# Experts in blocks of 1024 columns with deeper rings, and the low part of every weight chunk on VectorE alone

## The reference

```python
def _expert_choice_ffn(h, router_w, wg, wu, wd):      # per group; 16 experts, FF = 2048
    cap = EC_CAPACITY_FACTOR * n // N_EXPERTS         # 64 latent + 16 context rows per expert
    probs = jax.nn.softmax((h @ router_w).astype(jnp.float32), axis=-1)
    gate, idx = lax.top_k(jnp.swapaxes(probs, 1, 2), cap)
    xs = h[b_idx, idx]
    hid = silu(xs @ wg[e]) * (xs @ wu[e])
    ye = (hid @ wd[e]) * gate[..., None]
    return zeros_like(h).at[b_idx, idx].add(ye)
```

## Time and profile before

| what | us |
|---|---|
| median of three runs | 1772.27 (1772.03 to 1791.83) |
| the profiled execution | 1767.41 |
| its span, first to last instruction | 1765.4 |
| TensorE busy | 1557.6 |
| VectorE busy | 1235.6 |
| GpSimd busy | 1155.3 |
| ScalarE busy | 1000.3 |
| moved by DMA | 476.73 MB |

### The profile page before, as it was taken

One profiled execution on the slowest core, in us unless ns is written; L12 is line 12 of the kernel. 1 busy time (PEld: TensorE's weight loads), 2 busy tenths in 40 slices (PEclk: granted clock), 3 DMA queues, 4 the chain that ended last, 5 costly groups with the idle time before them and its releaser, 6 DMA issues.

```text
span 1765.4 us, 21080 instructions
## 1 busy us (share of the span) xinstructions
PE 1557.6 (88%) x7025; PEld 1059.3 (60%) x7025; DVE 1235.6 (70%) x1121; ACT 1000.3 (57%) x813; POOL 1155.3 (65%) x517
## 2 busy tenths in 40 slices
PE   5699987888848999999999999999999899999992
PEld 2588765556735556565656656566665565655661
DVE  5525554774565877788787877778878678887773
ACT  6223344243425666676766667667676676766761
POOL 5311231143116797897988989889797797977880
PEclk9699999989858999999999999999999999999996
DMA  9321113256225898999999999999999989989983
GB/s 343 105 72 48 48 49 98 84 174 236 106 107 214 325 357 316 347 348 342 364 344 367 342 339 361 335 377 339 341 376 333 354 329 350 363 330 357 335 317 126
DMA packets 189109, 476.73 MB, mean 270 GB/s; under 512 B 11406, under 2 KB 13706, under 8 KB 172684
## 3 DMA queue, kind: packets, MB, share of 16 engines
q1 hardware_dynamic: 177744, 447.77, 68.8%
q0 software_dynamic: 3728, 13.11, 3.0%
q10 hardware_dynamic: 7596, 15.30, 2.4%
HBM read 462.51 MB, written 13.64 MB: 270 GB/s over the span
## 4 chain that ended last, share of the span: by engine, by line
POOL 41%; issue 22%; PE 20%; DVE 7%; DMA 5%; ACT 4%; POOLq 0%; ACTq 0%; SPq 0%; DVEq 0%
POOL w_lo L256 37%; PE bank L287 3%; PE bank L288 3%; PE bank L286 3%; ACT w_hi L250 2%; POOL arena L1437 2%; DMA raw<-in_ada_w 2%; POOL gate_e L1433 1%; PE bank L852 1%; DVE w_lo L256 1%; PE bank L769 1%; PE bank L692 1%; DMA arena<-xn_rows,slot_e 1%; PE bank L899 1%; PE bank L900 1%
## 5 line engine op out<-in xcount | busy, mean ns | idle before, releaser
L256 POOL TENSOR_TENSOR w_lo<-raw,w_hi 128x384 fp32r<-128x384 f32 (+1 forms) x424 | 1032.1, 2453 | 512.5 <-ACT w_hi L250 507.6
L256 DVE TENSOR_TENSOR w_lo<-raw,w_hi 128x1664 fp32r<-128x1664 f32 (+1 forms) x424 | 902.3, 2139 | 379.0 <-ACT w_hi L250 376.8
L250 ACT CAST w_hi<-raw 128x2048 fp32r<-128x2048 f32 x424 | 806.5, 1910 | 340.8 <-PE bank L904 90.5
L899 PE MATMUL bank<-w_hi,act_lo 128*80 128x512 f32 x1024 | 410.9, 401 | 19.6 <-DVE act_lo L1337 19.5
L900 PE MATMUL bank<-w_hi,act_hi 128*80 128x512 f32 x1024 | 406.5, 397 | 0.0
L904 PE MATMUL bank<-w_lo,act_hi 128*80 128x512 f32 x1024 | 279.4, 394 | 3.9 <-POOL w_lo L256 3.7
L914 PE MATMUL bank<-w_hi,act_lo 128*80 128x512 f32 x512 | 204.3, 399 | 16.9 <-DVE act_lo L1348 13.8
L899 PEld LDWEIGHTS bank<-w_hi,act_lo 128*80 128x80 f32 x1024 | 155.9, 152 | 102.1 <-issue 21.9
L904 PEld LDWEIGHTS bank<-w_lo,act_hi 128*80 128x80 f32 x1024 | 151.8, 149 | 92.1 <-issue 9.8
L900 PEld LDWEIGHTS bank<-w_hi,act_hi 128*80 128x80 f32 x1024 | 153.8, 150 | 79.7 <-issue 2.8
L915 PE MATMUL bank<-w_hi,act_hi 128*80 128x512 f32 x512 | 201.1, 393 | 0.0
(11 more groups left out here) (208 smaller groups left out, 1400.9 us busy)
## 6 DMA issues: line engine op xcount, KB each, us to landing
raw<-in_exp_gate SPq DMA_DIRECT2D x128, 1024.0 KB, 5.4
raw<-in_exp_up SPq DMA_DIRECT2D x128, 1024.0 KB, 5.4
raw<-in_exp_down SPq DMA_DIRECT2D x128, 1024.0 KB, 5.8
raw<-in_ada_w SPq DMA_DIRECT2D x24, 1024.0 KB, 6.1
raw<-in_w_in SPq DMA_DIRECT2D x12, 1024.0 KB, 5.2
arena<-in_x_lat ACTq DMA_DIRECT2D x8, 512.0 KB, 9.1
raw<-in_w_out SPq DMA_DIRECT2D x4, 1024.0 KB, 7.5
xn_rows<-arena ACTq DMA_DIRECT2D x5, 512.0 KB, 2.7
```

The costliest lines, as they stand in the source:

```text
L250: nc.scalar.copy(w_hi[:, n % WS, :], raw[:, n % RAW, :]).then_inc(hi_done, 1)
L256: ops.tensor_tensor(w_lo[:, n % WS, at], raw[:, n % RAW, at], w_hi[:, n % WS, at], ALU.subtract).then_inc(done, 1)
L899: mm(dst, x[1][:, kk, :], wh[:, k, :], start=(kk == 0), stop=False)
```

## The change

1. `split_lo` is VectorE's alone, for all 2048 columns, in the prologue and in the experts. GpSimd keeps its other work there, and in the experts only copies columns, gathers and scatters.
2. For expert chunks the raw ring has 6 slots and the w rings 4. The added slots lie where xn2, h2T and the activations of the prologue are dead by then (`raw_more`, `w_hi_more`, `w_lo_more`); the fifth and sixth load wait for that.
3. The hidden width is worked in blocks of 1024: all expert chunks are two pieces x 1024 columns, in four parts per block. For gate and up the runs in memory become 4 KB instead of 2 KB. The body is now, four chunks each: g1 d0 u1 g0' d1 u0'. Gate uses banks 0 and 1, up 2 and 3, down 4 and 5.
4. All side work is placed anew. In the body of expert e, with chunks numbered 0 to 23 in that order: hidden transposes behind chunks 1, 2, 13 and 14; `gathered_T` behind chunks 4 and 7; `gathered` for the two halves behind VectorE's lo parts of chunks 9 and 12; ScalarE's `gathered_half` behind its hi parts of chunks 10 and 13; `gathered_lo` behind the lo parts of chunks 11 and 14; `ye` behind the hi parts of chunks 24 and 25 (0 and 1 of the next body). GpSimd does columns, gather and scatter with nothing between.

The number of matmuls, transposes and bytes stays as it is. The core of the diff follows: the constants, the order of chunks, loads and splits, then the bodies of TensorE, VectorE, ScalarE (its lines stand behind `split_hi(act, N_BODY + i + WS_X, e)`) and GpSimd.

```diff
 RAW, WS = 4, 3
+RAW_X, WS_X = 6, 4
-DVE_COLS, DVE_COLS_EXP = 1536, 1664
...
-        order = [("u", 1, 0), ("d", 0, 0), ("g", 2, 0), ("u", 2, 0), ("d", 1, 0), ("g", 3, 0), ("u", 3, 0), ("d", 2, 0)]
-        if not last:
-            order += [("g", 0, 1)]
-        order += [("d", 3, 0)]
-        if not last:
-            order += [("u", 0, 1), ("g", 1, 1)]
-        return [(kind, b, half, nxt) for kind, b, nxt in order for half in range(2)]
+        order = [("g", 1, 0), ("d", 0, 0), ("u", 1, 0)] + [("g", 0, 1)] * (not last) + [("d", 1, 0)] + [("u", 0, 1)] * (not last)
+        return [(kind, b, part, nxt) for kind, b, nxt in order for part in range(4)]
...
+        elif j == RAW:
+            sp_e.wait_ge(xn_out, 16 * TILES)
+            sp_e.wait_ge(h2_ps, 2 * TILES)
+        elif j == RAW + 1:
+            sp_e.wait_ge(sl_rd, 1)
+        else:
+            sp_e.wait_ge(lo_done, e * PER_E + (n - RAW_X + 1))
...
+        if n >= N_EXP + WS:
+            act.wait_ge(w_used, e * PER_E + (n - WS_X + 1))
...
+    def split_lo(dve, n, e=0):
+        dve.wait_ge(hi_done, e * PER_E + (n + 1))
+        nc.vector.tensor_tensor(w_chunk(w_lo, n), raw_chunk(n), w_chunk(w_hi, n), ALU.subtract).then_inc(lo_done, 1)
...
+                if part == 0:
+                    if kind == "g":
+                        pe.wait_ge(sl_ev, 4 * e + (4 if nxt else 2))
+                        if nxt:
+                            pe.wait_ge(xs_l, 2 * e + 4)
+                    elif kind == "u":
+                        pe.wait_ge(hid_rd, 4 * e + (4 if nxt else 2))
...
+                if kind == "g" and part in (1, 2):
+                    half = 2 * (1 - b) + part - 1
+                    if part == 2:
+                        pe.wait_ge(ht_lo, 4 * e + half)
+                    hid_T(e, half)
...
+                if not last and (kind, b, part) == ("d", 0, 0):
                     pe.wait_ge(xs_f, 2 * e + 2)
                     pe.wait_ge(xg_in, 16 * e + 32)
                     gathered_T(1 - pr2, 0)
+                if not last and (kind, b, part) == ("d", 0, 3):
                     pe.wait_ge(xs_f, 2 * e + 3)
                     gathered_T(1 - pr2, 1)
...
+                if kind == "u" and part == 3:
+                    for half in range(2):
+                        hidden(n, e, e + nxt, 2 * b + half)
...
+                if not last or i + WS_X < len(chunks):
+                    split_lo(dve, n + WS_X, e)
+                if not last and (kind, b, part) == ("d", 0, 1):
                     gathered(e + 1, 0)
+                if not last and (kind, b, part) == ("d", 0, 3):
                     gathered_lo(e + 1, 1 - pr2, 0)
+                if not last and (kind, b, part) == ("u", 1, 0):
                     gathered(e + 1, 1)
+                if not last and (kind, b, part) == ("u", 1, 2):
                     gathered_lo(e + 1, 1 - pr2, 1)
...
+                    if part == 2 and not last:
+                        gathered_half(e + 1, 1 - pr2, 0)
+                if not last and (kind, b, part) == ("u", 1, 1):
                     gathered_half(e + 1, 1 - pr2, 1)
+                if not last and (kind, b) == ("u", 0) and part < 2:
+                    ye_out(e, pr2, part, N_BODY + 19)
...
+            if not last:
+                pool.wait_ge(sl_ct, 1)
+                pool.wait_ge(ga_ps, 2 * e + 2)
+                pool.wait_ge(f_add, 16 * e + 16)
+                columns_of(e + 1, 1 - pr2, col_ct)
+                pool.wait_ge(sl_ct, 1)
+                pool.wait_ge(col_ct, 2 * e + 2)
+                gather(1 - pr2)
+            pool.wait_ge(sl_ct, 1)
+            pool.wait_ge(ye_rd, 2 * e + 2)
```

More of the change, by code:

```diff
@@ new lines, in body_chunks, with raw_chunk, w_chunk @@
+        return [(kind, b, part, nxt) for kind, b, nxt in order for part in range(4)]
+    FIRST_CHUNKS = [(kind, 0, part) for kind in "gu" for part in range(4)]
+    def raw_chunk(n):
+        if n < N_EXP:
+            return raw[:, n % RAW, :]
+        slot = (n - N_EXP) % RAW_X
+        return raw[:, slot, :] if slot < RAW else raw_more[slot - RAW]
+    def w_chunk(ring, n):
+        if n < N_EXP:
+            return ring[:, n % WS, :]
+        slot = (n - N_EXP) % WS_X
+        if slot == WS:
+            return w_hi_more if ring is w_hi else w_lo_more
+        return ring[:, (N_EXP + slot) % WS, :]
@@ L559, in _ @@
         split_hi(act, N_EXP + 2)
+        split_hi(act, N_EXP + 3)
         act.wait_ge(lg_sub, 1)
@@ L826, in _ @@
             chunk_ready(pe, n)
-            wh, wl = chunk_view(w_hi, n, 512), chunk_view(w_lo, n, 512)
+            wh, wl = cols(w_chunk(w_hi, n), 512), cols(w_chunk(w_lo, n), 512)
             for t in range(TILES):
@@ L890, in gathered_T, with products @@
             last.then_inc(ga_ps, 1)
-        def up_or_gate(n, e, bank, half, x):
-            dst = psum[bank][0:SLOTS, :]
-            wh, wl = chunk_view(w_hi, n, 512), chunk_view(w_lo, n, 512)
+        def products(n, e, banks, x, first, final):
+            wh, wl = cols(w_chunk(w_hi, n), D), cols(w_chunk(w_lo, n), D)
+            steps = [(j, q, slice(q * 512, (q + 1) * 512)) for j in range(2) for q in range(2)]
             pe.wait_ge(hi_done, e * PER_E + (n + 1))
-            for k in range(4):
-                kk = 4 * half + k
-                mm(dst, x[1][:, kk, :], wh[:, k, :], start=(kk == 0), stop=False)
-                mm(dst, x[0][:, kk, :], wh[:, k, :], start=False, stop=False)
+            for j, q, at in steps:
+                dst = psum[banks + q][0:SLOTS, :]
+                mm(dst, x[j][1], wh[:, j, at], start=(first and j == 0), stop=False)
+                mm(dst, x[j][0], wh[:, j, at], start=False, stop=False)
@@ L922, in hid_T, with up_or_gate, down @@
+        def up_or_gate(n, e, kind, part, x):
+            products(n, e, 0 if kind == "g" else 2, [[a[:, 2 * part + j, :] for a in x] for j in range(2)],
+                     part == 0, part == 3)
+        def down(n, e, b, part):
+            at = [slice((2 * (part % 2) + j) * SLOTS, (2 * (part % 2) + j + 1) * SLOTS) for j in range(2)]
+            products(n, e, 4, [[a[:, at[j]] for a in hidT[part // 2]] for j in range(2)],
+                     b == 0 and part == 0, b == 1 and part == 3)
         def hid_T(e, b):
@@ new lines, in body @@
+                if kind == "g" and part in (1, 2):
[3 more added lines that the diff above has]
+                    hid_T(e, half)
+                if last and (kind, b, part) == ("u", 1, 3):
+                    hid_T(e, 2)
+                    pe.wait_ge(ht_lo, 4 * e + 3)
+                    hid_T(e, 3)
+                if last and (kind, b, part) == ("d", 1, 1):
+                    pe.wait_ge(gbias2, 16)
+                    pe.wait_ge(sl_ev, 4 * NEXP)
+                    pe.wait_ge(hid_rd, 4 * NEXP)
+                    gate_rows(rows, (0, 1, 2, 3))
@@ L1371, in body @@
[L1371 to L1382 removed]
+            if last:
+                gate_row(4, (0, 1, 2, 3))
```

287 lines of the change are left out of this document (117 added, 170 removed).

## The result

The changed kernel is slower: 1825.59 us (median of four runs, 1818.35 to 1833.31) against 1772.15 before; the recorded ratio is 1.032, with a 95% interval of 1.027 to 1.037 (the two medians alone give 1.030). The forecast was 1765 us, with 1730 to 1792 as its range. The profiled execution took 1826.2 us, its span 1824.4: 59.0 more than before. The times in the table of experiments are medians over all executions, while the ratios leave out one slow execution of e2 (1783.7 us) and one of e8 (3897.3 us, without which its median is 1796.4).

The account below looks back on a forecast made before the run. TensorE was taken as the bound, 69.2 us per expert. With waits and clock 74.2 against 74.4: -3 over 15 experts, prologue -4, tail +1, giving 1761 from 1767.4; the run median lies 0.3% higher: 1765 us, range 1730 to 1792.

Parts of the forecast that it names:

- TensorE's floor: Expert loop: 24 chunks of matmuls plus six transpose sets bound each expert at 69.2 us.
- VectorE alone: Low parts wholly on VectorE: 2.29 us per chunk, 62 us per expert of 72 or more, so not the bound.
- the prologue: Before the expert loop: GpSimd's low parts fall away, VectorE's grow; sum -4 us, bounds -9 and +6.
- Waits at L1348: TensorE's waits for the low activations of hid, 12.5 us in the loop before; the new order removes them.
- First half of the gathered rows: TensorE's wait in each expert for VectorE to split this half: 0.5 us.
- Second half: TensorE's wait in each expert for the other half of the gathered rows: 2.95 us, or 2.3 without backlog.
- The clock: Slowed TensorE matmuls after a long wait: 1.1 us per expert (6 in 10 of 1.9), bounds 0 and 1.9.
- The gather: Rows for the next expert land in time by 1.7 us at the medians; 0.5 us per expert, bounds 0 and 3.2.
- t21: End of chunk 21 on TensorE; from it the gather was timed to land after 18.1 us, 18.6 with semaphores and start.
- The late case: Scatter and gather at longest landing plus 0.6 for a busy queue: rows come 3.2 us after TensorE wants them.
- The rival with the late gather: Gather comes late and the clock falls at both waits: 79.7 us per expert, 1848 us; chance 0.12.
- The floor of 72.1 us: DMA's estimated time per expert by the skill page's 358 GB/s; the forecast preferred 67.4 us from a measured 383 GB/s.

Follow-up runs that it names:

- e2: Changed kernel with each expert load issued as two, giving 2 KB runs for gate and up: 1769.2 us, ratio 0.996.
- e8: Changed kernel with four raw slots instead of six and loads in 2 KB runs: 1798.1 us, ratio 1.012.
- e6: Changed kernel with the gather issued one body earlier, ahead of the scatter's wait, and gathered-row work one to two chunks earlier: 1687.4 us, ratio 0.949.
- e3: Kernel before the change with only VectorE doing all 2048 columns of every low part; old rings, blocks and order: 1737.4 us, ratio 0.979.
- e5: Changed kernel with the gather issued one body earlier from its own index buffer, ahead of the scatter's wait: 1729.1 us, ratio 0.973.
- e9g: Changed kernel with one load per expert held back until the gather has landed: 1774.3 us, ratio 1.003.
- e10: Changed kernel with every low part issued as two instructions of 1024 columns instead of one of 2048: 1792.9 us, ratio 1.012.

## Why the prediction was wrong

- **TensorE's floor** of 69.2 us per expert was right: 68.80 in e6.
- **VectorE alone** at 2.29 us per chunk was right (2290 ns), and so was that VectorE doesn't bound the expert. What it frees was mis-sized. I took the prologue at -4; the first transposes came 5.1 us earlier, and 9.3 in e3. The 4 us between the two are the first gather: 519.25 to 527.20 in the changed kernel, 518.82 to 523.01 in e3, where no fifth and sixth load is issued at that point. In the old order alone it also takes 1.5 us off an expert. I had no sum for this part by itself, which is worth 35 to 38 us.
- **Waits at L1348** went, as said, and no wait of ScalarE for raw is left in the expert stage.
- **First half of the gathered rows**, 0.5 us: it isn't there. In e5, where no gather wait could cover it, TensorE doesn't wait at its second transposes, and they start 8.60 us behind the first, as in e6 (8.59), where this work stands earlier.
- **Second half**, 2.95 us taken: 2.2 and 0.17 ahead of it, 2.37 measured, in each expert. The value without backlog, 2.3, was the right one.
- **The clock**, 1.1 us per expert taken, 0 to 1.9 as bounds. Alone, a wait of 2.2 us costs the clock in few experts (four periods of 14 in e5). In the changed kernel it did so each time, and 13 of the 14 gather waits did too. The bounds of the term allowed one fall per expert; there were two.
- **The gather**, 0.5 us taken, is the step that failed, by the two landings in its line from t21. Its other terms were right. ye's second half is written at 1023.46, 2.7 us behind t21 (1020.77, from TensorE's steps; 2.8 taken), the scatter starts 0.87 later (0.8 taken), from the copies to the gather it is 1.17 (1.2 taken). For the landings I took 7.6 + 6.5 = 14.1; in this cycle they are 9.60 (1024.33 to 1033.93) and about 10.0 (1035.10 to just ahead of 1045.18): 5.5 more. With 14.1 TensorE would have had 1.5 us to spare (2.7 + 0.9 + 14.1 + 1.2 = 18.9 behind t21; it comes at 20.44, 1041.21). The difference, 4.0, is the wait of 3.97. The sign that I had named for this, a gather wait above 1 us, came.
- **A slip in the same line.** Its own terms, 2.8 + 0.8 + 7.6 + 1.2 + 6.5, add up to 18.9 and not to 18.1, and with the 0.5 for semaphores and start to 19.4: the slack was 0.9 us, not 1.7. The late case then is 4.0 us after TensorE and not 3.2, and the upper bound of the term was too low by as much; measured are 4.3 us on average in the loop. The slip alone would have left the gather in time at the medians; it hid how thin the margin was.
- **Why the landings were mis-sized.** I took them from a kernel in which GpSimd did low parts, and held them to be free of what this change alters. The runs put the gather's 3.5 us down to 0.3 for the instruction and 3.2 behind it; of these 2.0 are loads issued beside it (e9g takes them away). 2 KB runs give 1.2 (e2), which may be partly the same. For the scatter 0.7 of 2.2 are the instruction. Some 1.2 and 1.5 us stay open. My argument against this rival, that both medians were taken beside a full queue, was wrong in its first half: from the gather's start on no load went out for 3.6 to 4.5 of its 6.5 us.
- **The rival with the late gather** gave 79.7 us per expert and 1848; measured are 78.7 and 1826. It was the case that came, at a chance of 0.12, and by its own point: over 1.7 us above the medians. Its mechanism was right (landings at the longest seen or above, clock falling twice). That its number is so near is in part luck: it took 0.5 us that aren't there and 2.95 for 2.37, and had the gather's wait at 3.2 for 4.3. Its chance should have been far larger, since even the slack of 1.7 was 12% of a sum of times that were all seen with another engine setting the pace.
- Two rules of the Trainium skill stood beside the forecast. The floor of 72.1 us estimated from the first (DMA: Bandwidth & Descriptors, "Where 436 GB/s comes from") doesn't hold here: e6 runs at 68.80 us and 376 GB/s. So DMA was not the bound, as taken. The oscillating clock (TensorE: Matmul & The Clock Gate, "HAM oscillation") is what the changed kernel shows; in e5, with one wait in every iteration, the clock fell in four of 14.

## What to carry to other kernels

A landing time is a property of the kernel it was taken in. When an engine that paced the loads is relieved, other loads come to lie beside a small transfer; they were 2.0 of the gather's 3.5 us here. A chain whose slack is smaller than that wants a margin for it. Look at the chain itself first: a gather whose indices are known long before has no business behind a scatter, and moving it gave 96 us; the deeper ring was worth its 52 us only once TensorE waited for nothing, the longer runs nothing then. Take a change apart before judging it: its first part alone was worth 2.1%, the remainder cost 5% on top of it, and with both waits repaired the whole is 5.1% faster than before.

## What I hadn't expected of the hardware

- GpSimd's DMA_INDIRECT takes 1.00 us with VectorE idle, 2.4 to 3.1 beside one low part of 2048 columns, and 5.5 beside two; in three kernels (changed, e5, e10) it ended 0.87 to 0.88 us behind the end of a VectorE instruction.
- A scatter-add of 80 rows takes 9.2 to 10.1 us to land in every variant with the new order, whatever ring, runs or held loads, against 7.2 before (medians).
- One core moved 376 GB/s over 940 us and 399 over 20 us (e6).
- A TensorE wait of 2.2 us, the same in every expert, cost the clock in four of 14 periods in e5 and in each of the changed kernel, where, but for the first, a wait of 3 to 7.5 us lay 22 to 24 us ahead of it.
